# Two attention blocks on one core: the gating's layer norm moved into the second attention's rounds, its product and the gate row moved behind the last weighted sum, and the first attention's sum ordered by memory halves

## What is computed

```python
# first block: memory cross attention
scores = jnp.einsum("bshd,bmhd->bhsm", q, k) / math.sqrt(XHEAD_DIM)
probs = jax.nn.softmax(scores, axis=-1)
o = jnp.einsum("bhsm,bmhd->bshd", probs, v).reshape(bsz, s, D_MODEL)      # the weighted sum over 256 memory rows
...
# second block
y_a = _swa_with_sinks(q, k, v, sinks[l]) * jax.nn.silu(z_a)
vn = _layernorm(gelu(v_b), ln_g, ln_b).reshape(b, nc, CHUNK, N_GROUPS, GROUP_W)
w = jnp.where(causal[None], w_s, 0)
sv = jnp.einsum('gts,bnsgc->bntgc', w, vn) + b_s.T[None, None, :, :, None]
y_b = gelu(u_b) * sv.reshape(b, s, D_B) * jax.nn.silu(z_b)
gates = jax.nn.sigmoid(g_logits)                                          # 16 tiles of 128 features
merged = gate_a * (y_a @ w_proj_a[l]) + gate_b * (y_b @ w_proj_b[l])
x = x + gate * _rms(merged @ w_out[l], g_post[l])                         # gate: a row of 1024 numbers
```

## Time and profile before

| | |
|---|---|
| time, median of 3 runs | 1412.94 us (1411.88 to 1413.27) |
| the profiled execution's own time | 1413.47 us |
| its span, first to last instruction | 1412.2 us |
| PE (TensorE's matmuls) busy | 1393.5 us, 99% |
| DVE busy | 814.5 us, 58% |
| ACT busy | 479.1 us, 34% |
| POOL busy | 136.8 us, 10% |

### The profile page before, as it was taken

How to read it: one execution, slowest core, us unless ns; L and a number is a source line. 1 busy time by engine, 2 the same in 40 slices (tenths; PEclk the granted TensorE clock), 3 DMA queues, 4 the chain that set the end, 5 groups by cost and what they waited for, 6 DMA issues and landing times.

```text
span 1412.2 us, 20873 instructions
## 1 busy us (share of the span) xinstructions
PE 1393.5 (99%) x8982; PEld 1112.5 (79%) x8982; DVE 814.5 (58%) x1134; ACT 479.1 (34%) x723; POOL 136.8 (10%) x138
## 2 busy tenths in 40 slices
PE   7999999999999999999999999999999999999998
PEld 5687887878778888887778888887887877888886
DVE  7374654746548755354575674556635435767754
ACT  6332324234135333234431221323243232443323
POOL 1020302002002011001210000000040011003000
PEclk9999999999999999999999999999999999999999
DMA  5110201111042333322255543232221333212262
GB/s 190 59 46 32 76 32 60 47 46 61 32 164 90 105 120 119 105 75 75 90 179 194 194 164 101 93 97 93 86 100 65 98 97 104 90 61 75 79 174 90
DMA packets 42205, 136.18 MB, mean 96 GB/s; under 512 B 4650, under 2 KB 8362, under 8 KB 42113
## 3 DMA queue, kind: packets, MB, share of 16 engines
q1 hardware_dynamic: 33984, 114.57, 24.9%
q0 software_dynamic: 4080, 14.68, 2.8%
q10 hardware_dynamic: 4048, 5.59, 1.1%
HBM read 130.37 MB, written 2.10 MB: 94 GB/s over the span
## 4 chain that ended last, share of the span: by engine, by line
PE 95%; DVE 2%; DMA 1%; ACT 1%; issue 1%; ACTq 0%; DVEq 0%
PE bank L417 93%; PE bank L420 2%; DMA w_raw<-panels 1%; DVE opA_lo L1426 1%; DMA xT<-x 1%; DVE w_lo L1418 0%; DVE tmp L1426 0%; ACT scores L928 0%; DVE P L1426 0%; ACT w_hi L928 0%; DVE scores L1418 0%; ACT opA_hi L928 0%; DVE tmp L1418 0%; DVE x_tokens L1426 0%; DVE pad L1418 0%
## 5 line engine op out<-in xcount | busy, mean ns | idle before, releaser
L1418 DVE TENSOR_TENSOR w_lo<-w_raw,w_hi 128x1024 fp32r<-128x1024 f32 (+1 forms) x209 | 257.4, 1232 | 348.0 <-ACT w_hi L928 347.7
L417 PE MATMUL bank<-opA_hi,w_hi 128*128 128x512 f32 x1000 | 410.8, 411 | 10.2 <-DVE opA_lo L1426 8.2
L417 PE MATMUL bank<-opA_hi,w_lo 128*128 128x512 f32 x1000 | 395.7, 396 | 0.0
L417 PE MATMUL bank<-opA_lo,w_hi 128*128 128x512 f32 x1000 | 394.6, 396 | 0.0
L928 ACT ACTIVATE w_hi<-w_raw 128x1024 fp32r<-128x1024 f32 (+1 forms) x209 | 220.1, 1053 | 368.3 <-DMA w_raw<-panels 368.1
L417 PEld LDWEIGHTS bank<-opA_hi,w_hi 128*128 128x128 f32 x1000 | 188.1, 188 | 64.6 <-issue 16.4
L417 PEld LDWEIGHTS bank<-opA_hi,w_lo 128*128 128x128 f32 x1000 | 188.3, 188 | 45.6
L417 PEld LDWEIGHTS bank<-opA_lo,w_hi 128*128 128x128 f32 x1000 | 188.5, 189 | 41.6 <-issue 2.2
L417 PE MATMUL bank<-opB_hi,w_hi 128*128 128x512 f32 x448 | 178.5, 398 | 0.3 <-DVE w_lo L1418 0.3
L417 PE MATMUL bank<-opB_hi,w_lo 128*128 128x512 f32 x448 | 177.2, 395 | 0.0
L417 PE MATMUL bank<-opB_lo,w_hi 128*128 128x512 f32 x448 | 177.2, 395 | 0.0
(11 more groups left out here) (317 smaller groups left out, 1624.5 us busy)
## 6 DMA issues: line engine op xcount, KB each, us to landing
w_raw<-panels SPq DMA_DIRECT2D x208, 512.0 KB, 3.3
ada_w<-ada POOLq DMA_DIRECT2D x24, 512.0 KB, 4.5
xT<-x ACTq DMA_DIRECT2D x1, 2048.0 KB, 14.5
x_tokens<-x_blocks SPq DMA_DIRECT2D x16, 128.0 KB, 4.0
out<-x_tokens SPq DMA_DIRECT2D x8, 256.0 KB, 2.0
memT<-mem ACTq DMA_DIRECT2D x1, 1024.0 KB, 5.7
xT<-x ACTq DMA_DIRECT2D x3, 256.0 KB, 7.5
xT<-x SPq DMA_DIRECT2D x3, 256.0 KB, 7.3
```

What stands on the lines that cost most here:

```text
L417: return pe.matmul(o, lhsT, rhs, start=start, stop=stop, skip_group_check=True)
L1418: return ve.tensor_tensor(o, a, b, op)
```

## The change

In the first attention the weighted sum runs over the memory half first and the feature half second, and each memory half waits only for the copy that it reads.

In the second block:

- DVE makes the gating's mean and variance during the `zb` panels, and ACT the root ahead of the first round. DVE's reciprocal follows.
- The norm itself is two SCALAR_TENSOR_TENSOR for each token tile, (v - mean) * gain and then * 1/std + bias, all on DVE; tiles 0 and 1 in round 1, tiles 2 and 3 in round 2, between the softmax's product and the next steps.
- TensorE turns `w_s` in round 1 behind the turns of the probabilities; DVE masks it in round 2.
- TensorE makes the gating's product right behind round 3's weighted sum and the gate row right behind that; all 42 remaining steps follow.
- DVE makes two gating groups, six steps, two more groups, the gate row's copies, then the rest; ACT's high parts and sigmoids are spread anew.
- POOL multiplies `ub` by `zb` as soon as each `zb` tile has left its bank, and has no part in the norm.

```diff
-F2_MAX, F2_SOFTMAX, F2_OUT, F2_LAST = 8, 10, 3, 14
-F2_COPY, F2_NORM, F2_SIGMOID = 6, 8, 7
+F2_MAX, F2_SOFTMAX, F2_OUT = 8, 10, 3
+F2_GATING, F2_SIGMOID = 6, 7
-F2_MID = 16 * KT - 2 - 4 * (F2_MAX + F2_SOFTMAX + F2_OUT) - F2_LAST
+F2_LAST = 16 * KT - 2 - 4 * (F2_MAX + F2_SOFTMAX + F2_OUT)
...
# TensorE, first attention
-            pe.wait_ge(pt_v, h + 1)
-            pe.wait_ge(pt_a, h + 1)
-            for mt in range(2):
-                evicted("kv", KT + 2 * h + mt)
             if h:
                 pe.wait_ge(op_lo, OPERAND["xo"] + 2 * h)
-            for d in range(2):
-                for mt in range(2):
+            for mt in range(2):
+                pe.wait_ge((pt_v, pt_a)[mt], h + 1)
+                evicted("kv", KT + 2 * h + mt)
+                for d in range(2):
                     c = h * XD + d * NP
                     ins = mm(bank[6 + d][:, :], vtm[:, mt, c:c + NP], pT[n][:, mt, :], mt == 0, mt == 1)
-                ins.then_inc(weigh_mm, 1)
+                    if mt:
+                        ins.then_inc(weigh_mm, 1)
...
# TensorE, second attention, behind a round's turns
+            if t == 1:
+                pe.wait_ge(gating_here, 64)
+                pe.wait_ge(sv_step, 1)
+                for g4 in range(4):
+                    ins = turn(bank[6][:, g4 * NP:(g4 + 1) * NP], wsr[:, g4, :])
+                ins.then_inc(ws_mm, 1)
             p.steps(F2_OUT)
...
# TensorE, behind the rounds
-        pe.wait_ge(gating_here, 64)
-        pe.wait_ge(op_lo, OPERAND["merge2"] + 3)
-        for g in range(4):
-            ins = turn(bank[6][:, g * NP:(g + 1) * NP], wsr[:, g, :])
-        ins.then_inc(ws_mm, 1)
-        p.steps(F2_MID)
         pe.wait_ge(vn_v, 4)
-        pe.wait_ge(vn_g, 4)
-        pe.wait_ge(ws_done, 1)
         for g in range(4):
             ...
             ins.then_inc(sv_mm, 1)
-        p.steps(F2_LAST)
-        pe.wait_ge(ws_done, 1)
         pe.wait_ge(sv_step, 4)
         for k in range(KT):
             ...
         ins.then_inc(ws_mm, 1)
+        p.steps(F2_LAST)
         p.to("out2")
...
# ACT, ahead of the rounds
         p.to("gates2")
+        ac.wait_ge(bn_step, 9)
+        act(mv[:, :, 1:2], mv[:, :, 1:2], ACT.Sqrt).then_inc(root_done, 1)
...
# ACT, behind the rounds
+        gated_high(0)
+        gated_high(1)
+        p.steps(F2_GATING)
+        gated_high(2)
+        gated_high(3)
+        p.steps(2 * F2_SIGMOID - F2_GATING)
         sigmoids(range(0, 4))
         p.steps(F2_SIGMOID)
         sigmoids(range(4, 8))
-        p.steps(F2_MID - F2_COPY - F2_NORM - F2_SIGMOID)
-        for g in range(4):
-            ac.wait_ge(sv_step, 4 + 2 * g + 2)
-            act(opB[0][:, 4 + g, :], tmp[g % 2][:, :], ACT.Copy).then_inc(op_hi, 1)
+        p.steps(F2_LAST - 4 * F2_SIGMOID)
+        sigmoids(range(8, 12))
         p.steps(F2_SIGMOID)
-        sigmoids(range(8, 12))
-        p.steps(F2_LAST - F2_SIGMOID)
...
# POOL, behind the rotary products
+        for g in range(4):
+            i = FIRST["zb"] + g
+            gp.wait_ge(left[i % 2], left_after(i))
+            tt(P[:, UB + g, :], P[:, UB + g, :], P[:, ZB + g, :], ALU.mult).then_inc(uz_done, 1)
...
# DVE, in the zb panels
+        for n in range(4):
+            ve.wait_ge(vb_made, n + 1)
+            ve.bn_stats(st6[:, n, :], vn[:, n, :]).then_inc(bn_step, 1)
+            ve.wait_ge(bn_step, 2 * n + 1)
+            ve.bn_aggr(mv[:, n, :], st6[:, n, :]).then_inc(bn_step, 1)
+            if n == 1:
+                p.steps(KT)
+        ve.wait_ge(bn_step, 8)
+        ts(mv[:, :, 1:2], mv[:, :, 1:2], 1.0, ALU.mult, EPS, ALU.add).then_inc(bn_step, 1)
...
# DVE, the rounds
+        def value_norm(n):
+            ve.wait_ge(bn_step, 10 + n)
+            ve.wait_ge(gating_here, 64)
+            stt(vn[:, n, :], vn[:, n, :], mv[:, n, 0:1], lng[:, :], ALU.subtract, ALU.mult).then_inc(bn_step, 1)
+            ve.wait_ge(bn_step, 10 + n + 1)
+            stt(vn[:, n, :], vn[:, n, :], mv[:, n, 1:2], lnb[:, :], ALU.mult, ALU.add).then_inc(vn_v, 1)
...
             tt(sc[:, :, 0:256], sc[:, :, 0:256], rs.unsqueeze(2).broadcast_to([NP, 8, 256]),
                ALU.mult).then_inc(prob_done, 1)
+            if t == 2:
+                ve.wait_ge(ws_mm, 1)
+                tt(wst[:, :, :], bank[6][:, :].rearrange("p (g t) -> p g t", g=4), wide("causal", 4),
+                   ALU.mult).then_inc(ws_done, 1)
+            if t in (1, 2):
+                value_norm(2 * t - 2)
+                value_norm(2 * t - 1)
             p.steps(F2_SOFTMAX)
...
# DVE, behind the rounds: the whole norm is taken out here, and of the groups
             low_part(opB, 4 + g, tmp[j][:, :], OPERAND["merge2"] + 4 + g + 1)
-        p.steps(F2_LAST)
+            if g == 1:
+                p.steps(F2_GATING)
         ve.wait_ge(ws_mm, 2)
         for b in range(2):
             ve.tensor_copy(gate_row[:, b * S:(b + 1) * S], bank[6 + b][:, :]).then_inc(ws_done, 1)
+        p.steps(F2_LAST - F2_GATING)
```

More of the change, by code:

```diff
@@ L406, in build @@
     assert N_PANELS == panels.shape[0], (N_PANELS, panels.shape)
-    sink_done, bn_step, ws_mm, ws_done, vn_v, vn_g, uz_done, sv_mm, sv_step = (
+    sink_done, bn_step, ws_mm, ws_done, vn_v, uz_done, sv_mm, sv_step = (
         sem("sinks_spread"), sem("batch_norm_step"), sem("w_s_turned_then_gate_row"), sem("w_s_masked_then_gate_row"), sem("v_normed_vector"),
-        sem("v_normed_pool"), sem("uz_made"), sem("gating_multiplied"), sem("gating_step"))
+        sem("uz_made"), sem("gating_multiplied"), sem("gating_step"))
     x3_here = sem("x3_here")
@@ L858, in tensor_program @@
             pe.wait_ge(pt_v, XH + 2 * t + 2)
+            if t == 2:
+                pe.wait_ge(ws_done, 1)
             first = [True, True]
@@ L1235, in scalar_program @@
             act(opB[0][:, t, :], P[:, ZA + t, :], ACT.Copy).then_inc(op_hi, 1)
-        p.steps(F2_COPY + F2_NORM)
-        ac.wait_ge(bn_step, 9)
-        act(mv[:, :, 1:2], mv[:, :, 1:2], ACT.Sqrt).then_inc(root_done, 1)
         def sigmoids(ms):
@@ L1245, in sigmoids, with gated_high @@
                 act(P[:, G2 + m, :], P[:, G2 + m, :], ACT.Sigmoid).then_inc(gate_done, 1)
+        def gated_high(g):
+            ac.wait_ge(sv_step, 4 + 2 * g + 2)
+            act(opB[0][:, 4 + g, :], tmp[g % 2][:, :], ACT.Copy).then_inc(op_hi, 1)
+        gated_high(0)
[4 more added lines that the diff above has]
+        p.steps(2 * F2_SIGMOID - F2_GATING)
         sigmoids(range(0, 4))
@@ L1404, in gpsimd_program @@
                            sinkb[:, 2 * t:2 * t + 2].unsqueeze(1).broadcast_to([NP, 4, 2])).then_inc(sink_done, 1)
[L1405 to L1412, removed]
     def vector_program():
@@ L1920, in vector_program @@
         mx, nm, su, rs = (stat2[:, 8 * q:8 * q + 8] for q in range(4))
+        ve.wait_ge(root_done, 5)
+        ve.reciprocal(mv[:, :, 1:2], mv[:, :, 1:2]).then_inc(bn_step, 1)
+        def value_norm(n):
[4 more added lines that the diff above has]
+            stt(vn[:, n, :], vn[:, n, :], mv[:, n, 1:2], lnb[:, :], ALU.mult, ALU.add).then_inc(vn_v, 1)
         ve.wait_ge(sink_here, 32)
@@ L1954, in vector_program @@
             low_part(opB, t, P[:, ZA + t, :], OPERAND["merge2"] + t + 1)
[L1956 to L1979, removed]
         for g in range(4):
```

## The result

| | median | runs | lowest to highest |
|---|---|---|---|
| before | 1412.31 us | 7 | 1411.59 to 1413.27 |
| after | 1416.67 us | 7 | 1415.90 to 1418.99 |

The ratio is 1.0032, with an interval of 1.0020 to 1.0043: slower, by 4.4 us. Forecast were 1416.0 us in a range of 1413.6 to 1419.2, and slower as the likeliest. The sign held, the time lies in the range, and the size was 3.0 forecast against 4.4 measured; most of the difference is a mechanism that the forecast had as a rival.

A forecast was written before the change was run, and what follows sets the result against it. TensorE, 99% busy, was taken as the bound, with DVE's lateness paid in full. 2.90 + 1.77 - 0.31 - 0.98 - 0.34 = +3.04 us on a median of 1412.94 gave 1416.0 us, range 1413.6 to 1419.2.

The forecast's parts named there:

- The bound and the frame: TensorE, 99% busy: only its own work and waits count; the work is unchanged, and late DVE deliveries are paid in full.
- Round 1, +2.90: DVE's norm of two tiles delays the copy of panel 3, so TensorE starts panel 5 later: 2.90 us lost.
- Round 2, +1.77: Mask and two norm tiles on DVE delay w_lo, panel 6's copy and probs_t: 1.77 us lost on TensorE.
- First attention, -0.31: Last head's weighted sum starts after DVE's half alone, without waiting for ACT's probs_t: 0.31 us gained.
- Gating's product, -0.98: TensorE's wait for POOL's vn_g before the gating's product goes, as the norm is finished earlier: 0.98 us gained.
- fewer changes of kind, -0.34: In the tail, sum, product and gate row become one f32 stretch, saving switches on TensorE: 0.34 us gained.
- The covers: Moved statistics, root, POOL products and tail gating groups stay hidden at no cost; the tail has 1.8 us to spare.
- the thin cover: ACT's root and DVE's reciprocal finish before DVE's first score instruction, with 0.2 us to spare.
- rival (4): Tail: gating groups take 3.4 us instead of 2.71, so their cover fails; 1.0 us more, 1417.0 us; chance 8%.
- rivals (2): DVE's additions are hidden and only the gains stay, 1411.3 us; decided at panel 5; chance 6%.
- (3): Losses only half: round 2's wait mostly vanishes or new instructions take 0.5 us; 1413.9 us; chance 12%.
- The clock, rival (1): TensorE's clock falls to half rate in round 1's wait, costing up to 3.3 us, 1.7 likelier: 1418.5; chance 22%.

The follow-up runs named there:

- round 2 alone: Changed kernel with norm tiles 0 and 1 moved behind round 1's probs_t copies, tiles 2, 3 and mask left in round 2: 1412.19 us, ratio 1.0001.
- the norm behind the copies: Changed kernel with norm tiles 0, 1 behind round 1's probs_t copies, 2, 3 behind round 3's, mask behind round 2's: 1410.70 us, ratio 0.9990.
- the filler: Three f32r matmuls behind each of three one-column groups at the first block's end, added to the norm behind the copies: 1411.65 us, ratio 0.9994.

## Why the prediction was right, and where it was off

**The bound and the frame.** That whatever DVE delivers late is paid in full holds. That TensorE's waits alone count does not: its instructions are the same, but 1.5 us of the loss lie in instructions that take longer at half clock. The 0.7 us by which busy time went down hide this, because before's profile has the longer fall near 1060.

**Round 1, +2.90.** Exact: the norm takes 2.90 us on DVE, and the wait at panel 5 went from 0.41 to 3.31. The price from one form of another line (748 ns) was right at 0.74 to 0.75, and so was the way in which the four overlap, 0.67 and 0.78 from start to start. The 2.66 us by VectorE: DVE Perf Modes of the Trainium skill, section The TRN2 errata, would have been 0.24 short.

**Round 2, +1.77.** 1.74 in the profile, and again 1.74 with round 2 alone. Panel 8's wait was forecast at about 1.2 and is 1.22; behind it I forecast 0.4 for `probs_t`, and it is 0.22, booked as "issue".

**First attention, -0.31.** 0.30, with and without the rest of the change. The wait is put down to "issue", where I had written that it would be DVE's copy.

**Gating's product, -0.98, and fewer changes of kind, -0.34.** Together they were mis-sized. The tail is 1.45 us shorter (39.82 to 38.37), and the turns of `w_s`, which stand in round 1 now, have to come off. From round 1's turns to the next f32r matmul it is 2.10 us with them (1231.13 to 1233.23, the norm behind the copies, clock at 1.00) and 1.66 without (before, 1232.82 to 1234.48): 0.44. That leaves 1.01 instead of 1.32. The product takes 3.67 (1282.98 to 1286.65) and the gate row 3.50, where they took 3.57 and 3.49: I had counted on 0.08 less, and there is 0.11 more. If the wait for `vn_g` was worth its 0.98, the fewer changes of kind brought next to nothing in place of 0.34. How the 1.01 is divided between the two is not shown; no run takes away one of them alone.

**The covers.** All held. In the profile after, ACT's root runs from 1195.17 for 0.21 us and DVE's reciprocal at 1195.41, and DVE's first score instruction at 1195.82 still waits 0.23 us for TensorE: the thin cover, given as 0.2, was 0.23 (the reciprocal takes 0.18). No wait comes in the tail, so rival (4) is out; rivals (2) and (3) are out by the 3.31 us and the 1.74.

**The clock, rival (1), at 22%.** This is the step that failed. I wrote that none of the shorter waits showed a fall and took that as evidence against one of 3.3 us. It came, and a wait of 1.86 us brought it too. So the sum put at nothing a term that is 1.5 us long, the largest of its errors. Its price as a rival was given as up to 3.3, 1.7 if half fell in waits; the profiles have 1.53 and 1.64. TensorE: Matmul & The Clock Gate of the Trainium skill, in its part on the HAM clock gate, has the rule that an engine left idle drops to half its rate until it has been busy again, and here the traces agree: 0.50 after the wait, 1.00 again 3.4 us later.

**The sum.** 2.90 + 1.74 - 0.30 - 1.01 = 3.33, and 1.5 for the clock: 4.9. Between the profiles, the fall near 1060 that only before's shows takes off 2.60: 3.33 + 1.53 - 2.60 = 2.3 against 2.4. Between the medians it is 4.4, with an interval of 2.8 to 6.1; how often and how long each kernel's runs had a fall is not known. That the forecast of 1416.0 came within 0.7 us of the time is in part luck: I added to a median of three runs, 1412.94, where seven give 1412.31. With that base my sum would have said 1415.4, and the missing clock would have stood out more.

## What to carry to other kernels

Before work is moved to an engine that has time on average, look up what stands behind the new place in that engine's order: the same four instructions cost 2.9 us of waiting and 1.5 of clock ahead of a copy that TensorE waits for, and nothing behind it, where DVE waits for TensorE. A wait of TensorE costs more than its length when the clock falls behind it, so price both. And when two profiles differ by less than some 3 us, look in both whether the clock fell at the same places before the difference is read as the change's.

## What the runs showed of the hardware

- A wait of 1.86 us on TensorE was enough for the granted clock to fall to 0.50, in some executions of one kernel and not in others. Behind the waits of up to 1.2 us in rounds 1 and 2 no profile here shows a fall.
- A stretch in which TensorE counts as busy can have the fall too: near 1060, behind or in some 3.5 us of one-column matmuls, seven of the ten profiles here have it, with a start between 1058 and 1062 and a length of 3 to 7 us. The changed kernel's and that of round 2 alone don't, and neither does the one with the filler there. It is worth 1.0 to 2.6 us (8.37 to 9.99 for the stretch against 7.37) and makes most of the spread of the runs: 2.6 us without filler matmuls, 0.8 with them.
- SCALAR_TENSOR_TENSOR of 128x512 in float32 with a per-partition number takes 0.75 us on DVE; the next starts 0.08 us before its recorded end if it doesn't need it, and 0.03 to 0.04 behind that end if it does.
